# Stage entries of a two-block transformer kernel: token tiles scaled, then transposed, with the turns in other places

## The reference

```python
# first block: every part reads a normalised x and adds a normalised result
x = x + 0.5 * rms_norm(swiglu_ffn(rms_norm(x, g_pre[0]), w1_in, w1_out), g_post[0])
x = x + rms_norm(token_mixer(rms_norm(x, g_pre[1]), ...), g_post[1])      # HGRN2 and mLSTM heads
x = x + 0.5 * rms_norm(swiglu_ffn(rms_norm(x, g_pre[2]), w2_in, w2_out), g_post[2])
# second block: no norm behind the parts
h = h + 0.5 * swiglu(rms_norm_2(h, g3), w3_in, w3_out)
h = h + merged_attention(rms_norm_2(h, g4)) @ w_out                        # MLA and stick-breaking
h = h + 0.5 * swiglu(rms_norm_2(h, g5), w4_in, w4_out)
h = h + sigmoid(rms_norm_2(h, g6) @ w_ple_gate) * (p @ w_ple_proj)
```

## Time and profile before

| | |
|---|---|
| median of three runs | 2386.91 us |
| the profiled execution | 2389.54 us |
| its span, first to last instruction | 2387.9 us |
| PE busy | 2314.7 us, 97% |
| POOL busy | 1320.8 us, 55% |
| DVE busy | 816.6 us, 34% |
| ACT busy | 448.7 us, 19% |
| mean granted clock of PE | 0.986 |

### The profile page before, as it was taken

One profiled execution on the slowest core, in us unless ns is written; L12 is line 12 of the kernel. 1 busy time (PEld: TensorE's weight loads), 2 busy tenths in 40 slices (PEclk: granted clock), 3 DMA queues, 4 the chain that ended last, 5 costly groups with the idle time before them and its releaser, 6 DMA issues.

```text
span 2387.9 us, 26080 instructions
## 1 busy us (share of the span) xinstructions
PE 2314.7 (97%) x11060; PEld 1905.6 (80%) x11060; DVE 816.6 (34%) x838; ACT 448.7 (19%) x736; POOL 1320.8 (55%) x772
## 2 busy tenths in 40 slices
PE   6999999999999999999999999999988999999999
PEld 6888888887778888888888888777656788888887
DVE  2323104884244333104323104420567632333013
ACT  3111003323222111003111002111268121111011
POOL 4666665634156666665666665566114656666654
PEclk9999999999799999999999999999899999999999
DMA  4333332211123333332333332223000223333322
GB/s 158 97 97 97 97 97 71 80 54 54 36 80 97 97 97 97 97 97 72 97 97 97 97 97 84 85 88 99 27 1 1 73 86 97 98 97 100 104 86 82
DMA packets 55580, 201.05 MB, mean 84 GB/s; under 512 B 6409, under 2 KB 6537, under 8 KB 55337
## 3 DMA queue, kind: packets, MB, share of 16 engines
q1 hardware_dynamic: 53712, 193.62, 26.4%
q10 hardware_dynamic: 1752, 5.77, 0.6%
HBM read 197.27 MB, written 2.10 MB: 83 GB/s over the span
## 4 chain that ended last, share of the span: by engine, by line
PE 88%; DVE 6%; ACT 3%; issue 1%; DMA 1%; POOL 1%; ACTq 0%; DVEq 0%; POOLq 0%
PE psum L360 19%; PE psum L361 18%; PE psum L362 18%; PE psum L420 7%; PE psum L422 7%; PE psum L421 7%; PE psum L400 1%; PE psum L565 1%; ACT junk L1145 1%; DVE x L1629 1%; PE psum L1069 1%; PE psum L620 1%; PE psum L1071 1%; PE psum L1070 1%; PE psum L458 1%
## 5 line engine op out<-in xcount | busy, mean ns | idle before, releaser
L325 POOL TENSOR_TENSOR w_lo<-w_raw,w_hi 128x1024 fp32r<-128x1024 f32 (+1 forms) x365 | 891.3, 2442 | 30.5
L323 POOL TENSOR_SCALAR w_hi<-w_raw 128x1024 fp32r<-128x1024 f32 (+1 forms) x365 | 388.4, 1064 | 909.9 <-PE psum L362 659.9
L360 PE MATMUL psum<-u_hi,w_hi 128*128 128x512 f32 (+1 forms) x2072 | 795.3, 384 | 10.8 <-DVE work L1977 4.7
L361 PE MATMUL psum<-u_hi,w_lo 128*128 128x512 f32 (+1 forms) x2072 | 789.9, 381 | 0.0
L362 PE MATMUL psum<-u_lo,w_hi 128*128 128x512 f32 (+1 forms) x2072 | 789.4, 381 | 0.0
L360 PEld LDWEIGHTS psum<-u_hi,w_hi 128*128 128x128 f32 x2072 | 392.6, 189 | 90.2 <-issue 7.8
L362 PEld LDWEIGHTS psum<-u_lo,w_hi 128*128 128x128 f32 x2072 | 392.4, 189 | 74.5
L361 PEld LDWEIGHTS psum<-u_hi,w_lo 128*128 128x128 f32 x2072 | 392.8, 190 | 73.6 <-issue 0.7
L420 PE MATMUL psum<-w_hi,hidden_hi 128*128 128x512 f32 x800 | 311.8, 390 | 1.0 <-DVE work L1836 1.0
L421 PE MATMUL psum<-w_lo,hidden_hi 128*128 128x512 f32 x800 | 311.2, 389 | 0.0
L422 PE MATMUL psum<-w_hi,hidden_lo 128*128 128x512 f32 x768 | 298.8, 389 | 0.0
(11 more groups left out here) (269 smaller groups left out, 1735.6 us busy)
## 6 DMA issues: line engine op xcount, KB each, us to landing
w_raw<-in_ffn_in SPq DMA_DIRECT2D x176, 512.0 KB, 3.5
w_raw<-in_ffn_out SPq DMA_DIRECT2D x88, 512.0 KB, 3.5
w_raw<-in_proj_in SPq DMA_DIRECT2D x34, 512.0 KB, 3.5
w_raw<-in_mix_in SPq DMA_DIRECT2D x29, 512.0 KB, 3.5
w_raw<-in_embed SPq DMA_DIRECT2D x10, 512.0 KB, 3.5
w_raw<-in_mix_out SPq DMA_DIRECT2D x8, 512.0 KB, 3.4
w_raw<-in_branch SPq DMA_DIRECT2D x8, 512.0 KB, 3.6
w_raw<-in_proj_out SPq DMA_DIRECT2D x8, 512.0 KB, 3.5
```

The costliest lines, as they stand in the source:

```text
L323: pool.tensor_scalar(hi, raw, 1.0, 1.0, ALU.mult, ALU.mult).then_inc(k.w_split, 1)
L325: pool.tensor_tensor(lo, raw, hi.bitcast(F32), ALU.subtract).then_inc(k.w_split, 1)
L360: pe.matmul(out, hi[:, cols], xhi, start=first, stop=False)
L361: pe.matmul(out, lo[:, cols], xhi, start=False, stop=False)
```

## The change

Three things, in one edit:

1. DVE no longer makes a diagonal. It multiplies the whole token tile by the inverse root, 128 x 1024, into a part of `work` that is free then (`scaled_tile`), and PE turns it with eight transposes against the identity.
2. On PE, the pair-0 half of the first chunk stands ahead of the turn of tile 2; it stood behind it. From stage 4 on (`EARLY`), the turns of tiles 0 and 1 stand within the output products of the stage before: ahead of the last 12 of the 18 products of tile 3.
3. On DVE and ACT, the roots and u_hi/u_lo of the first features change places with the update and the square of tiles 2 and 3.

```diff
+EARLY = 4

+def scaled_tile(k, i):
+    return k.big[:, (8 + 2 * i) * T:(10 + 2 * i) * T]

 def pe_turn_tile(k, s, i):
-    pe = k.nc.tensor
-    pe.wait_ge(k.x_diag, NT * s + i + 1)
+    pe, x = k.nc.tensor, scaled_tile(k, i)
+    pe.wait_ge(k.x_scaled, NT * s + i + 1)
     if s and i in (0, 2):
         wait_out_taken(k, pe, s - 1, i + 1)
     for t in range(KD):
         c = TURN_BANK[i // 2] * T + (2 * t + i % 2) * P
-        m = pe.matmul(k.psum[:, c:c + P], x_tile(k, i)[:, t * P:(t + 1) * P], k.diag[:, i * P:(i + 1) * P], start=True, stop=True)
+        m = pe.transpose(k.psum[:, c:c + P], x[:, t * P:(t + 1) * P], k.cst(C_ID))
     m.then_inc(k.x_turned, 1)

 def pe_enter(k, s, name, c0=0, c1=1):
-    pe_turn_tile(k, s, 0)
-    pe_turn_tile(k, s, 1)
+    if s < EARLY:
+        pe_turn_tile(k, s, 0)
+        pe_turn_tile(k, s, 1)
+    pe_dense_half(k, s, name, c0, CHUNK_BANK[0], 0)
     pe_turn_tile(k, s, 2)
-    pe_dense_half(k, s, name, c0, CHUNK_BANK[0], 0)
     pe_turn_tile(k, s, 3)
...
@@ pe_out
     for step, (i, part) in enumerate(steps):
         for kk in part:
+            if step == 5 and kk == tail[1] and st + 1 >= EARLY:
+                pe_turn_tile(k, st + 1, 0)
+                pe_turn_tile(k, st + 1, 1)
...
@@ pe_embed
-    pe_turn_tile(k, 6, 0)
-    pe_turn_tile(k, 6, 1)
-    pe_turn_tile(k, 6, 2)
     pe.wait_ge(k.u_lo, 2 * KD * 6 + 4)
     gate(0, 0, (0, 1))
+    pe_turn_tile(k, 6, 2)
     pe_turn_tile(k, 6, 3)
     gate(0, 1, (0, 1))
...
@@ act_out
-        else:
+        elif i < NT - 1:
             act_square_updated(k, st, i)
-    if st < 3:
-        act_hi(k, s, 0, range(4))
-        act_square_updated(k, st, NT - 1)
-        act_hi(k, s, 0, range(4, KD))
-    else:
-        act_hi(k, s, 0)
+    act_hi(k, s, 0, range(4))
+    act_square_updated(k, st, NT - 1)
+    act_hi(k, s, 0, range(4, KD))
     act_hi(k, s, 1)

@@ dve_root_x
-    dve.tensor_scalar(k.diag[:, i * P:(i + 1) * P], k.cst(C_ID), r, None, ALU.mult).then_inc(k.x_diag, 1)
+    dve.tensor_scalar(scaled_tile(k, i), x_tile(k, i), r, None, ALU.mult).then_inc(k.x_scaled, 1)

 def dve_out(k, st):
     s = st + 1
-    for i in range(NT):
-        if st < 3:
+    if st < 3:
+        for i in range(NT):
             dve_post(k, st, i)
             if i:
                 dve_root_x(k, s, i - 1)
+            if i == NT - 1:
+                dve_lo(k, s, 0, range(2))
             dve_update(k, st, i)
-        else:
-            dve_update(k, st, i)
-            dve_root_x(k, s, i)
-    if st < 3:
+        dve_lo(k, s, 0, range(2, 4))
+    else:
+        dve_update(k, st, 0)
+        dve_update(k, st, 1)
+        dve_root_x(k, s, 0)
+        dve_root_x(k, s, 1)
+        dve_update(k, st, 2)
+        dve_root_x(k, s, 2)
+        dve_update(k, st, 3)
         dve_lo(k, s, 0, range(4))
-        dve_root_x(k, s, NT - 1)
-        dve_lo(k, s, 0, range(4, KD))
-    else:
-        dve_lo(k, s, 0)
+    dve_root_x(k, s, NT - 1)
+    dve_lo(k, s, 0, range(4, KD))
     dve_lo(k, s, 1)
```

More of the change, by code:

```diff
@@ L177, in __init__ @@
         self.eps_set, self.x_inv, self.y_inv = sem("eps_set"), sem("x_inv"), sem("y_inv")
-        self.x_diag, self.x_turned, self.u_hi, self.u_lo = sem("x_diag"), sem("x_turned"), sem("u_hi_done"), sem("u_lo_done")
+        self.x_scaled, self.x_turned, self.u_hi, self.u_lo = sem("x_scaled"), sem("x_turned"), sem("u_hi_done"), sem("u_lo_done")
         self.norm_var, self.norm_root, self.norm_inv = sem("norm_var"), sem("norm_root"), sem("norm_inv")
```

## The result

The changed kernel takes 2397.27 us (median of 12 runs, 2388.60 to 2400.23), the kernel before 2386.90 us (12 runs beside them, 2385.71 to 2390.41). The ratio is 1.0039 [1.0031, 1.0048]: slower by 0.4%, more than the 0.2% that counts here as a difference. Forecast were 2390, in a range of 2380 to 2398. The time is inside the range, but 7.3 us above the forecast and nearest to rival A's value (2395).

A forecast was written before the change was run, and what follows sets the result against it. PE works 97% of the span but waits for DVE and ACT at stage entries. Terms gave -2.5 us at full clock, +3.0 with the clock: 2392.5 from the profiled 2389.5, 2390 as median; range 2380 to 2398.

The forecast's parts named there:

- rival A: Entries 4 to 6: tile 3's scaling loses its turn to POOL, 2.2 us each in 4 and 5; 2395, chance 0.25.
- Transposes: PE turns: eight transposes of 0.11 us replace 16 instructions, a tile falling from 1.78 to about 0.88 us.
- Whole-tile scaling: DVE scaling 1024 instead of 128 columns: 0.75 us instead of 0.29 with POOL idle, up to 2.4 us more beside POOL.
- The 31.1 us: All waits in front of the turns were said to sum to 31.1 us, 17.7 of them the kernel's start.
- Entries 1 to 3 at full clock: First three entries after the start: 0.9 us longer each, PE idle 6.3 us, since PE was not what was late.
- Half clock in all six entries: Entries 1 to 6: longer PE idle drops the clock, costing about 0.5 us in entries 1 to 5, 1.9 in 6.
- First product of entry 4: PE's products start at 1465.5 instead of 1467.00, 1.5 us earlier, after 2.8 us idle.
- DVE is ahead by some 0.2 us: Entries 4 and 5: DVE asks to scale tile 3 at 1466.86, POOL's L325 at about 1467.1; 0.2 us gained each.
- Rival A's own condition: Entries 4 and 5: the turn is lost once tile 3's scaling asks later than POOL's L325 does.
- Entry 0: Start of the kernel: 2.0 us earlier from cheaper turns, between -2.0 and 0 with the clock, taken as -1.0.
- Rival C: Transposes do not raise PE's clock, so entry 0 gains nothing and half clock lasts longer; 2393, chance 0.13.

The follow-up runs named there:

- f5: Changed kernel plus small products nothing reads (filling) in PE's idle spans ahead of the first products of entries 1 to 6; 2389.65 us, 1.0015 of before.
- f6: e3 plus filling with small unread products in PE's idle spans (24 in entries 1 to 3, then 9 and 11); 2389.16 us, 1.0003 of before.
- g1: Changed kernel, but ACT instead of DVE scales tile 3 in entries 4 to 6; 2387.57 us, 1.0000 of before.
- after: The changed kernel itself, all three parts of the edit against the kernel before; 2397.27 us, 1.0039 of before.
- e3: Changed kernel with the turns of tiles 0 and 1 back at the entry in stages 4 to 6 (EARLY = 7); 2393.40 us, 1.0027 of before.
- e4: Changed kernel; in entries 4 to 6 tile 3 is squared and scaled after two features instead of four; 2397.72 us, 1.0043 of before.
- e1: Kernel before with whole-tile scaling and transposes alone, every order as before; 2396.56 us, 1.0036 of before.
- g4: f6 with transposes as the filling, two for each small product; 2390.18 us, 1.0012 of before.
- g2: f7 plus filling in PE's idle spans, early turns of tiles 0 and 1, and ACT scaling tile 3 in entries 4 to 6; 2380.08 us, 0.9968 of before.
- e2: Changed kernel with diagonals and products for the turns again, keeping the new order; 2405.89 us, 1.0081 of before.
- f7: e3 with entries 1 to 3 put back as in the kernel before (diagonals, products, old order); 2384.02 us, 0.9994 of before.
- g3: Kernel before with filling alone: 8 and 5 small unread products in PE's idle spans of entries 1 to 3; 2381.21 us, 0.9979 of before.

## Why the prediction was right in its range and wrong in its case

- **Transposes.** Right: 0.11 us each at full clock, 16 in 1.91 us with the last one's tail (entry 0), so 0.88 us a tile or a little less. Right too that they are hidden in entries 1 to 3, where PE was not late.
- **Whole-tile scaling.** Right: 0.75 us alone (entry 0), 1.02 to 2.95 us where it meets POOL.
- **Two readings of rows.** The 31.1 us of the earlier trace rows count PE's weight loads too; PE's own waits in front of the turns were 24.1 us. And the first window of the earlier trace rows prints a granted clock of 1.00, because the clock's record begins only at 22.3 us. That it was the half level is seen from the instructions: 21 in 4.60 us there, and 17 in 1.70 us from 22.3 on. No term of the sum changes by either.
- **Entries 1 to 3 at full clock.** +0.9 each was forecast, f5 and f6 measured +0.93; the idle ahead of the products was 6.05 us, not 6.3.
- **Half clock in all six entries.** Right, in part by luck: behind the same idle the clock stayed full in entry 6 of g1. In 1 to 3 its cost was 0.0 to 0.7 us (after against f5), forecast 0.5. In entry 6 it cost 2.85 us, forecast 1.9: all 12 products ran at half clock (5.29 us against 2.84 in f5), and the start of the turns made the other 0.4.
- **First product of entry 4.** Right: 1.5 us earlier by the same account. Idle ahead of it 2.78 us, forecast 2.8.
- **The step that failed:** "DVE is ahead by some 0.2 us", in entries 4 and 5. It was ahead by 0.03 and 0.01 us of POOL's start, and POOL went first. The term for these two entries was +0.3 each; measured were +3.2 and +4.1 against before. With ACT doing the scaling (g1) they shrink by 3.1 and 2.8 us, and in e3, where DVE is 0.43 us ahead, they are 0.3 us shorter than before. This is rival A, given 0.25. Its 2.2 us for the turn alone fit the estimate of 2.5 above; what it lacked is that the second half of the products, and some of the turns, also run at half clock behind the hole.
- **Rival A's own condition** was that the scaling asks later than L325. It lost though it began earlier by the records. Over these kernels tile 3's scaling lost with a lead of 0.01 to 0.04 us over POOL (five cases, after and f5), both lost and won at 0.05 (e4: lost in entries 4 and 6, won in entry 5), and won at 0.06 (f5, entry 6) and 0.43 (e3). So the turn tips at a recorded lead of about 0.05 us, finer than the steps that the prediction added up.
- **Entry 0.** -1.0 forecast, -0.9 measured, and that is luck: over the kernels with transposes it ended between 27.38 (e1) and 31.21 us (f5), against 30.52 before. The clock's record begins at 21.2 us in the one and at 30.0 in the other; what decides it stays open.
- **Rival C** was refuted as a mechanism by g4. The changed kernel's own entry 0 says the same: the granted clock was full from 20.83 us, when PE had done nothing but these transposes:

```profile
18.02 3.30 PE L407 MATMUL psum<-const,work 128*128 128x128 f32 x16 [18.02 <-DVE work L1589]
21.36 0.84 ACT L1177 ACTIVATE u_hi<-psum,param 128x256 fp32r<-128x256 f32 x2 [0.37 <-PE psum L407]
23.49 0.36 PE L367 MATMUL psum<-u_hi,w_hi 128*128 128x256 f32 x1 [2.17 <-DVE u_lo L1598]
```

- **The rest of the sum.** The steps give +10.3 us in entries 0 to 6; the attention mixer took 2.8 us less, with the same work, so the executions differ by 7.4. The prediction had no term for that stretch. That its number came within 7.3 us of the median owes something to it.

The theory formed on the result, that the lost turn alone explains the loss, did not hold either: e1 has no hole and is as slow. Two things cost, each some microseconds: a turn lost at POOL (4.2 us in each of entries 4 and 5, f5 against g2, some 1.7 of it half clock), and PE idle so long that the clock falls (3.3 us in entries 1 to 6 by the traces of after and f5, 2.3 by those of e3 and f6). Their parts overlap in entries 4 and 5. What f5's median gained beyond that, and g1's gains in entry 6 and the first mixer, the edits don't explain.

## What to carry to other kernels

Making an engine's work shorter where it waits anyway only lengthens its idle spans, and on PE such a span can be paid a second time at half clock (here from 2.1 us on); put unread work in it, or leave the slower form. Where a step rests on DVE being ahead of POOL by less than the error of your own account, price it as lost too, or give the step to ACT, as g1 did. Before crediting a few microseconds to an edit, compare a long stretch that it doesn't touch: here one moved by up to 7.9 us.

## What the runs showed of the hardware

- A DVE instruction that begins 0.01 to 0.04 us before POOL's still waits for all of it: 2.92 to 2.95 us for a scaling of 0.75. With 0.06 or 0.43 us it goes first, and POOL's takes 2.95 or 2.70 us instead of 2.35. A short one waits as well (e2: 1.67 us for 128 columns, 0.76 us behind POOL). ACT's scaling of the same tile beside a POOL instruction took 1.14 us. The Trainium skill (SBUF — State Buffer, Who interferes with whom) has the pair of ports that DVE and POOL share as an exclusive lock, with ACT outside it; these rows agree.
- The length of PE's idle span alone did not decide the clock in the entries. Behind spans of at most 1.5 us it never fell. Behind 2.12 to 2.14 (before, f7) it fell in one entry of three in each, behind 2.42 (e3, f7) in three of four, behind 2.75 to 3.09 in all, behind 3.12 and 3.13 (after, g1, e2) in one of three, behind 3.4 and more in all.
- The filling kept the clock at full wherever it filled PE's idle spans, transposes as well as products. The best kernel of this study is g2, 2380.08 us; g3 reaches 2381.21 by the filling alone.
